# A fourth seven-product step per group in the MLP, k and v, with two of VectorE's weight sums merged

## The reference, cut to what matters

```python
h = sqrelu_mlp(rmsnorm(x, norm_g[i, 2]), mlp_w1[i], mlp_w2[i])   # square(relu(x @ w1)) @ w2
...
proj = rms_norm(x, norm_g) @ w_in
q, k, v, z_a, u_b, v_b, z_b, g_a, g_b = split(proj, cuts)        # q, k, v: 1024 columns each
...
return x + merged @ w_out
```

## Time and profile before

| | us |
|---|---|
| median of 3 runs (1767.49 to 1768.45) | 1768.03 |
| the profiled execution, its own time | 1768.48 |
| its span | 1766.8 |
| PE busy | 1760.1 |
| DVE busy | 1352.2 |
| ACT busy | 912.5 |

### The profile page before, as it was taken

How to read it: one execution, slowest core, us unless ns; L and a number is a source line. 1 busy time by engine, 2 the same in 40 slices (tenths; PEclk the granted TensorE clock), 3 DMA queues, 4 the chain that set the end, 5 groups by cost and what they waited for, 6 DMA issues and landing times.

```text
span 1766.8 us, 26139 instructions
## 1 busy us (share of the span) xinstructions
PE 1760.1 (100%) x8758; PEld 1491.3 (84%) x8758; DVE 1352.2 (77%) x1814; ACT 912.5 (52%) x1269; POOL 143.5 (8%) x194
## 2 busy tenths in 40 slices
PE   9999999999999999999999999999999999999999
PEld 7888888888888888888888887888888888888887
DVE  6557777556788688878887877898888666885797
ACT  7434444446555445544554555767644454554453
POOL 1012222000000000100000000020003012000000
PEclk9999999999999999999999999999999999999999
DMA  9664454555567756765686576566555644565556
GB/s 326 201 219 162 166 166 157 189 178 189 172 212 226 204 188 214 227 201 190 206 235 195 189 222 223 189 204 210 191 189 179 198 160 167 191 201 192 179 191 191
DMA packets 99698, 348.43 MB, mean 197 GB/s; under 512 B 11536, under 2 KB 11936, under 8 KB 99232
## 3 DMA queue, kind: packets, MB, share of 16 engines
q1 hardware_dynamic: 93392, 333.23, 57.3%
q0 software_dynamic: 5360, 13.65, 3.7%
q10 hardware_dynamic: 864, 0.44, 0.1%
HBM read 336.77 MB, written 2.11 MB: 192 GB/s over the span
## 4 chain that ended last, share of the span: by engine, by line
PE 97%; DVE 2%; ACT 0%; POOL 0%; issue 0%; DVEq 0%; POOLq 0%
PE bank L508 23%; PE bank L487 23%; PE bank L492 12%; PE bank L802 11%; PE bank L804 11%; PE bank L803 11%; PE bank L558 1%; PE bank L524 1%; DVE w_lo L1687 1%; PE bank L637 1%; PE bank L680 1%; PE bank L695 1%; PE bank L686 0%; PE bank L679 0%; PE bank L696 0%; PE bank L608 0%
## 5 line engine op out<-in xcount | busy, mean ns | idle before, releaser
L1687 DVE TENSOR_TENSOR w_lo<-raw,w_hi 128x1024 fp32r<-128x1024 f32 x620 | 752.3, 1224 | 282.9 <-ACT w_hi L1103 278.4
L1103 ACT ACTIVATE w_hi<-raw 128x1024 fp32r<-128x1024 f32 x620 | 647.0, 1055 | 560.4 <-PE bank L508 185.2
L487 PE MATMUL bank<-h_both,w_hi 128*128 128x512 f32 x1792 | 432.6, 393 | 0.0
L487 PEld LDWEIGHTS bank<-h_both,w_hi 128*128 128x128 f32 x1792 | 330.4, 188 | 65.4
L492 PEld LDWEIGHTS bank<-h_both,w_lo 128*128 128x128 f32 x1792 | 229.8, 191 | 8.7
L492 PE MATMUL bank<-h_both,w_lo 128*128 128x256 f32 x1792 | 232.5, 283 | 0.0
L508 PE MATMUL bank<-w_hi,h_both 128*128 128x512 f32 x648 | 203.8, 396 | 0.0
L508 PE MATMUL bank<-w_hi,a_both 128*128 128x512 f32 x576 | 178.2, 391 | 0.0
L508 PEld LDWEIGHTS bank<-w_hi,h_both 128*128 128x128 f32 x648 | 119.7, 188 | 23.7
L802 PE MATMUL bank<-w_hi,h_both 128*128 128x512 f32 x328 | 128.3, 391 | 0.3 <-DVE w_lo L1687 0.2
L804 PE MATMUL bank<-w_lo,h_both 128*128 128x512 f32 x328 | 127.7, 389 | 0.0
(11 more groups left out here) (306 smaller groups left out, 2067.0 us busy)
## 6 DMA issues: line engine op xcount, KB each, us to landing
raw<-in_stream SPq DMA_DIRECT2D x622, 512.0 KB, 3.9
wide<-scaled POOLq DMA_DIRECT2D x21, 256.0 KB, 4.8
res<-in_x SPq DMA_DIRECT2D x4, 512.0 KB, 7.2
rowg<-in_norm_rows POOLq DMA_DIRECT2D x2, 1024.0 KB, 7.3
gate<-cum_rows POOLq DMA_DIRECT2D x1, 2048.0 KB, 7.7
wide<-gate POOLq DMA_DIRECT2D x7, 256.0 KB, 8.2
gate<-in_x_turned SPq DMA_DIRECT2D x5, 256.0 KB, 7.0
res<-gate POOLq DMA_DIRECT2D x4, 256.0 KB, 5.1
```

Source lines behind the costliest of these rows:

```text
L487: pe.matmul(tile_sum[b][:, :], w_hi[:, slot + half, k * P:(k + 1) * P], h_both[:, 8 * half + k, :], start=half == 0 and k == 0, stop=False)
L1103: nc.scalar.activation(w_hi[:, slot, :], raw[:, slot, :], ACT.Copy).then_inc(hi_ready, 1)
L1687: nc.vector.tensor_tensor(w_lo[:, slot, :], raw[:, slot, :], w_hi[:, slot, :].bitcast(F32), ALU.subtract).then_inc(lo_ready, 1)
```

## The change

It takes four steps in place of three in the MLP's seven groups and in k and v; q, the gates' and the output's groups keep three (the last one two). Steps of a four-step group stand at chunks 4, 6, 10 and 12. Of the steps at 6 and 12 the three form products are issued later, in the middle of chunk 8 and chunk 14, and DVE makes the forms' `lo` after three chunks' `lo` and not after two. The signs of the forms are changed: b12's place takes b12 + b11 (before: b12 - b11), form 0 is (b12 + b11) - b22, and forms 1 and 2 are b21 - form 0 and b11 - form 0 in one operation of 1024 columns; s3 has the other sign, and in `join_seven` two additions become subtractions. The activation forms get a fourth part, made in the MLP behind tile pair i = 7 and for q, k, v in `h_forms(0, 3)`, for which ACT has a fourth `h_forms_hi` ahead of `vb_in`. Some buffers move. SP's loop over the loads of chunks 16 and later is written out in full. Three pairs of semaphores are merged.

```diff
-PAIR_ORDER = (0, 1, 4, 2, 5, 3, 6, 7)
-SEVEN_PAIRS = (4, 5, 6)
-SEVEN_AT = (4, 8, 12)
+SEVEN_PAIRS = (4, 5, 6, 7)
+STEPS = len(SEVEN_PAIRS)
+PAIR_ORDERS = {2: (0, 1, 4, 2, 5, 3, 6, 7), 3: (0, 1, 4, 2, 5, 3, 6, 7), 4: (0, 1, 4, 5, 2, 6, 7, 3)}
+STEPS_AT = {2: (4, 8), 3: (4, 8, 12), 4: (4, 6, 10, 12)}
+FORMS_LATE = (6, 12)
...
+GROUP_STEPS = [STEPS] * WIDE_GROUPS + [3, 4, 4] + [3, 3] + [3, 2]
...
-            with sp.Fori(4, N_CHUNKS // RING) as j:
-                for slot in range(RING):
-
-                    sp.wait_ge(lo_ready, j * RING + (slot + 1 - RING))
-                    load(j * RING + slot, slot)
+            for c in range(4 * RING, N_CHUNKS):
+                sp.wait_ge(lo_ready, c + (1 - RING))
+                load(c, c % RING)
...
+            def wide_pairs(c, w, plain, seven, x, forms, x_formed, before_pair, before_seven, bank_free,
+                           after={}, late=None, chunks=WIDE_CHUNKS):
+
+                steps = {j: q for q, j in steps_of(w)}
+                held = []
+                for j in range(0, chunks, 2):
+                    pair = pair_at(w, j)
+                    before_pair(j, pair)
+                    if j in steps:
+                        before_seven(j)
+                        seven_blocks(c, j, steps[j], w, plain, seven, x, forms, x_formed)
+                        if GROUP_STEPS[w] == STEPS and j in FORMS_LATE:
+                            held.append(steps[j])
+                        else:
+                            form_products(steps[j], w, plain, seven, x, forms, late)
+                        continue
+                    for k in range(2):
+                        between = None
+                        if held:
+                            between = lambda q=held.pop(): form_products(q, w, plain, seven, x, forms)
+                        wide_chunk(c, j + k, 2 * pair + k, plain, x, bank_free, between)
...
+                late = FORMS_LATE if GROUP_STEPS[w] == STEPS else ()
+                for q, at in steps_of(w):
+                    if j + RING == at:
+                        act.wait_ge(form_step, 3 * (FIRST_STEP[w] + q) + 1)
+                next_split(WIDE_FIRST[w] + j)
+                for q, at in steps_of(w):
+                    if j + RING == at + (2 if at in late else 1):
+                        wide_form(w, q, forms)
...
-                nc.vector.tensor_tensor(s3, a11, a21, ALU.subtract).then_inc(x_form_step, 1)
+                nc.vector.tensor_tensor(s3, a21, a11, ALU.subtract).then_inc(x_form_step, 1)
...
+                nc.vector.tensor_tensor(b12, b12, b11, ALU.add).then_inc(form_step, 1)
+                dve.wait_ge(form_step, 3 * step + 1)
+                nc.vector.tensor_tensor(forms.w_raw[:, 0, :], b12, raw[:, c % RING + 1, GROUP_COLS:CHUNK], ALU.subtract).then_inc(form_step, 1)
...
+                dve.wait_ge(form_step, 3 * (FIRST_STEP[w] + q) + 2)
+                nc.vector.tensor_tensor(forms.w_raw[:, 1:3, :], raw[:, slot:slot + 2, 0:GROUP_COLS],
+                                        forms.w_raw[:, 0:1, :].broadcast_to([P, 2, GROUP_COLS]),
                                         ALU.subtract).then_inc(form_step, 1)
...
+                early = 3 if GROUP_STEPS[w] == STEPS and at in FORMS_LATE else 2
+                upto = steps[q + 1][1] if q + 1 < len(steps) else at + RING
+                second_form(w, q, forms)
                 if drain:
                     drain(0, 0)
-                inner_sum(step, at % RING, forms)
-                if drain:
                     drain(0, 1)
-                last_sum(step, at % RING, forms)
+                outer_forms(w, q, forms)
                 if drain:
                     drain(1, 0)
                     drain(1, 1)
-                for k in range(2):
-                    rest(c + at - RING + k, (at + k) % RING)
+                for k in range(early):
+                    next_rest(c + at - RING + k)
                     if between and k == 0:
                         between()
-                form_rest(step, forms)
-                for k in range(2, 4):
-                    rest(c + at - RING + k, (at + k) % RING)
+                form_rest(w, q, forms)
+                for k in range(at + early, upto):
+                    next_rest(c + k - RING)
...
-            h_forms(2)
+            h_forms(0, 2)
             next_rest(c + 11)
-            for q in range(STEPS):
-                h_forms_lo(q)
+            h_forms_lo(0, 0)
+            h_forms(0, 3)
+            for q in range(1, STEPS):
+                h_forms_lo(0, q)
```

More of the change, by code:

```diff
@@ L49 @@
 MOBA_LAST = 23
-OUT_STEPS = (3, 2)
+GROUP_STEPS = [STEPS] * WIDE_GROUPS + [3, 4, 4] + [3, 3] + [3, 2]
+FIRST_STEP = [sum(GROUP_STEPS[:w]) for w in range(len(GROUP_STEPS) + 1)]
+X_STEPS = (STEPS, 3, 3)
+X_FIRST = [sum(X_STEPS[:n]) for n in range(len(X_STEPS))]
 EPS = 1e-6
@@ L67 @@
 N_CHUNKS = sum(n for _, n in PHASES)
+WIDE_FIRST = [FIRST["mlp"] + 32 * (w // 2 + 1) + 32 * (w // 2) + 16 * (w % 2) for w in range(WIDE_GROUPS)]
+for _name, _at, _n in (("qkv", 16, QKV_WIDE), ("gates", 32, GATE_WIDE), ("out", 0, OUT_WIDE)):
+    WIDE_FIRST += [FIRST[_name] + _at + WIDE_CHUNKS * i for i in range(_n)]
 HEAD_CHUNKS = 16
@@ L820, in wide_chunk, with seven_blocks @@
                         mm.then_inc(half_group_done, 1)
+                    if between and t == 0:
+                        between()
                 mm.then_inc(chunk_done, 1)
-            def seven_products(c, j, q, w, plain, seven, x, forms, x_formed, steps=STEPS, late=None):
+            def seven_blocks(c, j, q, w, plain, seven, x, forms, x_formed):
                 kt = 2 * SEVEN_PAIRS[q]
                 slot = j % RING
-                first, last = q == 0, q == steps - 1
+                first, last = q == 0, q == GROUP_STEPS[w] - 1
                 def x_block(k, t):
@@ L844, in seven_products, with form_products, x_form, w_form @@
                 product(plain[1], x_form(3), w_block(slot + 1, 1)).then_inc(chunk_done, 1)
-                pe.wait_ge(form_lo_ready, STEPS * w + q + 1)
+            def form_products(q, w, plain, seven, x, forms, late=None):
+                first, last = q == 0, q == GROUP_STEPS[w] - 1
+                x_block = [part[:, 2 * SEVEN_PAIRS[q] + 1, P:TOK] for part in x]
+                def x_form(f):
+                    return [part[:, q, f, :] for part in (forms.x_hi, forms.x_lo)]
+                def w_form(f):
+                    return [part[:, f, :] for part in (forms.w_hi, forms.w_lo)]
+                pe.wait_ge(form_lo_ready, FIRST_STEP[w] + q + 1)
                 product(seven[3], x_form(2), w_form(1), first, last)
@@ L2024, in head_to_lo, with second_form @@
                                                 a_hi[:, kt, :].bitcast(F32), ALU.subtract).then_inc(head_ready, 1)
[L2026 to L2033 removed]
+            def second_form(w, q, forms):
+                step = FIRST_STEP[w] + q
+                c = WIDE_FIRST[w] + steps_of(w)[q][1]
+                for slot in (c % RING, c % RING + 1):
+                    dve.wait_ge(raw_landed[slot], 16 * (c // RING) + 16)
@@ L2737, in token_groups, with wide_groups @@
     return w.reshape(k // 256, 2, P, f // GROUP_COLS, GROUP_COLS).transpose(3, 0, 2, 1, 4).reshape(-1, P, CHUNK)
-def wide_groups(w):
-    order = [2 * p + k for p in PAIR_ORDER for k in range(2)]
-    return w.reshape(KT, P, -1, CHUNK).transpose(2, 0, 1, 3)[:, order].reshape(-1, P, CHUNK)
+def wide_groups(w, first):
+    groups = w.reshape(KT, P, -1, CHUNK).transpose(2, 0, 1, 3)
+    orders = [[2 * pair_at(first + n, j) + j % 2 for j in range(WIDE_CHUNKS)] for n in range(len(groups))]
+    return groups[[[n] for n in range(len(groups))], orders].reshape(-1, P, CHUNK)
 def paired_groups(w):
```

392 lines of the change are left out of this document (168 added, 224 removed).

## The result

The changed kernel takes **1786.67 us** (median of four runs, 1786.23 to 1788.67) against 1768.24 of the kernel before: a ratio of 1.0106, with a 95% interval of 1.0094 to 1.0118. It is slower, as forecast, but by 18 us and not by 11, and lies 1.7 us above the range. The profiled execution took 1786.23 us, its span is 1784.5.

The account below looks back on a forecast made before the run. PE bounds the kernel before; with four steps DVE would bound the wide groups. MLP 4.8, q 2.1, k and v 4.2, output -0.1 gave +11.0 (the 6.1 gain included) on 1768.48; less 0.45 for the median, 1779.0 us, range 1770 to 1785.

Parts of the forecast that it names:

- the sign and the mechanism: Whole kernel: slower by 11.0 us, since a fourth step fills DVE and PE waits for its `lo`; slower given 0.76.
- the faster rival: Nine wide groups: DVE keeps up and they run at PE's pace, 1762 us, or 1764 with q's loss; chance 10%.
- q: In front of q: the fourth activation form delays DVE and ACT, +2.1 us.
- the first step's start in w = 2: First group of a quarter: DVE begins the first step s = 5.68 us behind the group's start.
- the merged operation: Two outer sums as one DVE operation in each step: pitch 1.135 us, bounds 1.07 and 1.33.
- PE's gain: Nine groups lose three matmuls each, 27 x 0.2267 = 6.1 us; a four-step group lasts 40.8 us at PE's pace.
- s + 24.45 + 0.5 + 1.22 + 0.14 + 10.2: Length of a DVE-bound group, s + 36.5 us; s is when DVE begins the first step, counted from the group's start.
- the load: DVE's wait for chunk 11 in `raw` at a group's third step: 0.5 us, bounds 0 and 1.
- PE's stretch behind the stall: End of a four-step group: 45 matmuls behind the start of chunk 12 take 10.2 us.
- The second groups: MLP's second group in a quarter: s = 2.9, four drains add 2.27, length 41.7 us, +0.2 us, three times.
- w = 0: First quarter's first group: +2.1 us, with 1.4 from waiting for POOL and two tiny operations ahead of the first step.
- k and v: Groups k and v: DVE alone 41.1 us, ACT's pieces in the way 2.5, so 43.6; +2.1 us each, +4.2 together.

Follow-up runs that it names:

- the two cuts of DVE's work: Kernel after with the merged outer sum covering 64 of each 512 columns in four-step groups, 1769.03 us; or 256, with ACT's pieces moved, 1766.64 us.
- 2.1 us less a group: Kernel after with ACT's pieces in k and v moved and the merged outer sum covering 256 of each 512 columns in four-step groups: 1766.64 us.
- the pieces moved: Kernel after with ACT's twelve pieces (squares and scalings) in k and v moved to where ACT waits for DVE's next first sum: 1782.72 us, ratio 1.0081.

## Where the prediction was right, and where it was wrong

**Right:** the sign and the mechanism. PE is held at chunks 6 and 12 in the first groups and at 12 in the second ones, because a fourth step fills DVE, as the two cuts of DVE's work show. With 2.1 us less a group most groups reach PE's pace, where the faster rival has them, though with q's loss left no run came down to that rival's 1764. Also right in size: q, 2.2 for 2.1, where `vb_in` starts 3.4 us later than before apart from the MLP's delay of 9.5 (1130.77, and the row below) for 3.5 forecast; the first step's start in w = 2, the merged operation, PE's gain.

```profile
1143.65 0.67 ACT L1500 ACTIVATE gate<-bank,rstd 128x512 f32<-128x512 f32 x1
```

**The step that failed** is the length of a DVE-bound group, "s + 24.45 + 0.5 + 1.22 + 0.14 + 10.2". In w = 2 it gave 42.2, and 43.16 was measured. The missing 0.96:

- 0.42: a form's `lo` directly ahead of a first sum was priced at its pitch, 1.67, though the sum waits for this very `lo` and starts 1.88 behind it. Before the change two chunks' `lo` stood between them, so the wait was in no row, but it was in the code. It is an added wait that I did not count.
- 0.15: the load, 0.65 and not 0.5. In w = 3 it was 1.08. The bounds of 0 and 1 were about right.
- 0.11: the `lo` in front of that load wait counts with its duration, 1.22, and not with its pitch, since no next operation starts before its end (0.08), and rounding of the other pitches.
- 0.28: PE's stretch behind the stall. 45 matmuls at 0.2267 are 10.2 from start to start, but the group ends with the end of the last one, 0.39 behind its start: 0.16. The other 0.12 is the stall's own: from 694.83 the next ten matmuls take 2.39 us and not 2.27, the first 0.31 of it.

The second groups were 0.4 to 0.8 longer than forecast: the same terms, less what an earlier start gives back (in w = 3 the first step began at 2.3 and not at 2.9). w = 0 was 0.8 longer than forecast, much like the other first groups; that its end looks right, 2.2 for 2.1, is luck, by the 0.7 that PE was early. Without them the kernel would lie some 2.4 us above the range and not 1.7, an estimate from these rows.

**k and v** were forecast as DVE alone 41.1 and ACT 2.5. With the pieces moved they last 42.7, and ACT's order was worth 1.9. So ACT's part was 0.6 too large and DVE's 1.6 too small. That forecast had no term for a load in k and v. By estimate the load waits, 2.2 us for the two groups with the pieces moved, with the 0.42 and the 0.28 of above make 1.8 a group, about the 1.6; no run takes them apart. Two errors of opposite sign left the sum, 43.6, only 1.0 below the 44.6 measured.

**The range** ended at 1785 because it let only the load and the merged operation vary. Both behaved. What was off stood in terms that I took as certain, each by 0.1 to 0.4 us, and nine groups multiply it.

## What to carry to other kernels

When a change makes an engine the bound of a stage that repeats, build its chain instruction by instruction with every semaphore each one waits for, its own engine's included, since a neighbour that hid a wait may have been moved away; then give the range a term for what the chain leaves out, times the number of stages. Before freeing a full engine by giving its work to another, look at whether the two share a way to memory, and first try what costs nothing: waits put where the data is read, and a second engine's side work put where it waits anyway gave back 9.6 of 18 us here.

## What the runs showed that was not expected

- A second semaphore in the wait of a DVE operation costs 0.07 us even when it has long been fulfilled (0.72 to 0.79 or 0.80 between the sum and the form); a third 0.02 to 0.03.
- A POOL addition of 128x512 in SBUF takes 1.29 us where DVE's operation in front is just ending (688.03), and 1.92 where DVE is in the middle of one that reads two tensors from SBUF (684.45). Either way the next such operation of DVE takes up to 1.1 us longer. The rows look as if the two wait for each other in turn; no run tests that.
- Behind a stall PE's first matmul is followed after 0.30 or 0.31 us and the first ten take 2.37 to 2.40 us, where 2.27 is usual, at an unchanged granted clock of 1.00. It is so behind all twelve stalls of the MLP's groups, whether they last 0.20 or 1.71 us.
